# Expert stage of a decoder step: 34 passes of two 32-row half blocks, each with its own expert's weights, instead of 49 passes of one 64-row block

## The reference, cut to what matters

```python
def hier_moe(x, w_rg, b_rg, w_re, b_re, w_eg, w_eu, w_ed):   # x: 576 x 1024
    ...                                                      # group = argmax, then the best 2 of its 8 experts
    combine = jnp.sum(jax.nn.one_hot(eid, N_EXPERTS) * gate[..., None], axis=1)
    hg = jnp.einsum('nd,edf->nef', x, w_eg)                  # 32 experts, each 1024 x 256
    hu = jnp.einsum('nd,edf->nef', x, w_eu)
    hidden = jax.nn.silu(hg) * hu * combine[..., None]
    return jnp.einsum('nef,efd->nd', hidden, w_ed)           # 32 experts, each 256 x 1024
```

## Time and profile before

| | |
|---|---|
| median of 3 runs | 1352.9 us (1352.4 to 1355.35) |
| the profiled execution, its own time | 1347.98 us |
| its span, first to last instruction | 1346.0 us |
| PE busy | 1206.7 us, 90% of the span |
| mean granted TensorE clock | 0.952 |
| first transpose of the expert stage starts | 969.49 us |
| last down matmul of the stage ends | 1306.24 us |

### The profile page before, as it was taken

The page is one execution under the profiler, slowest core; times in us unless marked ns, Lnnn a source line. Parts: engine busy times, 40 slices in busy tenths (PEclk is TensorE's granted clock), DMA queues, the critical chain, the costliest instruction groups (busy, mean ns, idle before and its releaser), DMA issues.

```text
span 1346.0 us, 18797 instructions
## 1 busy us (share of the span) xinstructions
PE 1206.7 (90%) x7242; PEld 744.4 (55%) x7242; DVE 764.9 (57%) x1414; ACT 411.4 (31%) x852; POOL 570.2 (42%) x518
## 2 busy tenths in 40 slices
PE   5899999896798867788999899999998989999986
PEld 4435777685454533345666468877754545554432
DVE  1659999999888886887563134352522212221216
ACT  3630144543355465762222112231111111111110
POOL 5000096978775765757765000000233333443320
PEclk9999999998799978878999999998999999999998
DMA  9502222213565664757987320382299999999935
GB/s 329 193 28 67 63 82 76 81 52 98 148 174 167 185 191 133 252 168 250 328 266 267 133 99 32 102 323 76 84 418 413 409 395 364 366 415 416 403 113 206
DMA packets 92840, 281.46 MB, mean 209 GB/s; under 512 B 17960, under 2 KB 50552, under 8 KB 81800
## 3 DMA queue, kind: packets, MB, share of 16 engines
q1 hardware_dynamic: 54672, 165.64, 32.8%
q0 software_dynamic: 35520, 111.22, 24.7%
q10 hardware_dynamic: 2559, 3.40, 0.8%
HBM read 300.94 MB, written 23.11 MB: 241 GB/s over the span
## 4 chain that ended last, share of the span: by engine, by line
PE 49%; DVE 27%; DMA 11%; POOL 5%; issue 4%; ACT 4%; POOLq 0%; DVEq 0%; ACTq 0%; SPq 0%
PE ps L1526 9%; DVE arena L1962 6%; DVE arena L1961 5%; DVE arena L1963 5%; PE ps L1140 5%; PE ps L1550 5%; PE ps L1146 5%; POOL arena L1046 5%; PE ps L1370 4%; PE ps L1362 3%; DMA arena<-in_w_dn,arena 3%; PE ps L1228 2%; DMA arena<-scr_x,arena 2%; PE ps L1180 2%; DMA arena<-in_cache_kv,arena 2%
## 5 line engine op out<-in xcount | busy, mean ns | idle before, releaser
L1046 POOL DMA_INDIRECT arena<-in_cache_kv,arena x256 | 264.8, 1034 | 127.0 <-issue 73.7
L1140 PE MATMUL ps<-arena 128*128 128x288 f32 (+2 forms) x1120 | 294.8, 424 | 1.1 <-ACT arena L1694 1.1
L1140 PEld LDWEIGHTS ps<-arena 128*128 128x128 f32 (+1 forms) x1120 | 209.1, 189 | 84.4 <-issue 29.2
L1526 PE MATMUL ps<-arena 128*64 128x256 f32 x1568 | 189.7, 384 | 5.2 <-DMA arena<-in_w_gu 2.6
L1526 PEld LDWEIGHTS ps<-arena 128*64 128x64 f32 x1568 | 109.1, 138 | 83.8 <-issue 28.1
L1096 POOL DMA_INDIRECT scr_ypair<-arena x49 | 50.5, 1030 | 186.8 <-ACT arena L1896 168.1
L1089 POOL DMA_INDIRECT arena<-scr_x,arena x49 | 50.0, 1020 | 173.6 <-DVE arena L2343 159.0
L1617 ACT ACTIVATE arena<-ps 128x256 f32<-128x256 f32 (+5 forms) x138 | 57.9, 429 | 205.3 <-PE ps L1362 63.6
L1025 POOL TENSOR_TENSOR arena<-arena 128x816 f32<-128x816 f32 x58 | 103.0, 1775 | 17.5 <-ACT arena L1635 10.7
L1146 PE MATMUL ps<-arena 128*128 128x256 f32 (+4 forms) x544 | 107.0, 360 | 0.9 <-ACT arena L1839 0.6
L1550 PE MATMUL ps<-arena 128*64 128x512 f32 x392 | 98.9, 627 | 9.7 <-DMA arena<-in_w_dn,arena 9.7
(11 more groups left out here) (350 smaller groups left out, 1701.5 us busy)
## 6 DMA issues: line engine op xcount, KB each, us to landing
arena<-in_w_gu SPq DMA_DIRECT2D x32, 2048.0 KB, 12.5
arena<-in_w_dn SPq DMA_DIRECT2D x32, 1024.0 KB, 14.9
arena<-in_w_in SPq DMA_DIRECT2D x20, 1024.0 KB, 5.6
arena<-scr_q SPq DMA_DIRECT2D x32, 256.0 KB, 5.1
arena<-in_cache_kv,arena POOLq DMA_INDIRECT x256, 4.0
arena<-in_w_o SPq DMA_DIRECT2D x4, 1024.0 KB, 5.2
arena<-in_w_pg SPq DMA_DIRECT2D x4, 1024.0 KB, 9.2
arena<-scr_ypair SPq DMA_DIRECT2D x4, 1024.0 KB, 8.0
```

What stands on the lines that cost most here:

```text
L1046: pl.indirect_dma_start(unit_rows[:, 2 * j + t, half * H * HD:(half + 1) * H * HD], None, I["cache_kv"].rearrange("n (h d) -> (n h) d", h= ...
L1140: mm = nc.tensor.matmul(out, w[:, k], hT[:, k, a:b], start=(k == 0), stop=(k == KC - 1))
L1526: mm = nc.tensor.matmul(PS[2 + p % 2][64 * half:64 * half + 64, 0:2 * P], xT[:, p % 3, j, 64 * h:64 * h + 64], w[:, k, half, :], start=(k ...
```

## The change

The block shrinks from 64 to 32 rows, and one pass handles two blocks, each with its own weights. A block is now called a visit: 68 visits, two in each of 34 passes. There are six weight buffers of one whole expert each, and visit q always uses buffer q % 6, so pass p uses the pair (2p, 2p + 1) % 6. The blocks that are in use, sorted by expert, are numbered first, and each buffer gets a contiguous run of that numbering (`visit_blocks`): buffer 0 blocks 0 to 11, buffer 1 blocks 12 to 23, and so on. A visit whose expert is that of the visit before in the same buffer loads nothing. With these inputs 55 blocks are in use and 13 are empty.

Expert 0 is fetched early by SP into buffer 0 (one plain DMA instead of six). All other weights come by indirect DMAs of POOL, a whole expert each. Of the 68 such DMAs 32 move data, with these inputs. The number that move data in passes 0 to 33 is 1, 2, 1, 0, 2, 1, 0, 1, 1, 1, 1, 1, 1, 1, 1, 0, 0, 1, 1, 2, 1, 1, 2, 1, 0, 2, 1, 0, 1, 0, 2, 2, 0, 0. In passes 7, 9, 10, 12, 13 and 21 the one load is of the pair's second visit. (The list counts the experts that change within a buffer's run, from the rows above.)

```diff
-BLK = 64
-NOVER = (2 * N - NE) // (BLK + 1)
-NBLK = NE + NOVER
-XR = 6
+BLK = 32
+NSLOT = 6
+NBLK = -(-(2 * N + NE * (BLK - 1)) // BLK // 2)
+NVISIT = 2 * NBLK
+XR = 5
+XEARLY = 3
...
+def visit_blocks():
+
+    lengths = [len(range(j, NVISIT, NSLOT)) for j in range(NSLOT)]
+    return [sum(lengths[:q % NSLOT]) + q // NSLOT for q in range(NVISIT)]
...
                     sp.wait_ge(full, after("woS", 1))
-                    for e in range(3):
-                        load_expert(e)
-                    sp.dma_start(lng1, I["ln2_g"].rearrange("(a d) -> a d", a=1).to_broadcast([P, D])).then_inc(ln2_in, 16)
-                    sp.dma_start(lnb1, I["ln2_b"].rearrange("(a d) -> a d", a=1).to_broadcast([P, D])).then_inc(ln2_in, 16)
+                    sp.dma_start(eset[0], I["w_ex"][0:P, :]).then_inc(first_in, 16)
...
-            for e in range(3, NE):
-                sp.wait_ge(y_full, POS[("base", e - 3)] + 1)
-                load_expert(e)
...
+            def load_expert(q):
+                if q >= NSLOT:
+                    pl.wait_ge(y_full, (q - NSLOT) // 2 + 1)
+                elif q == 0:
+                    pl.wait_ge(first_in, 16)
+                pl.indirect_dma_start(eset[q % NSLOT], None, I["w_ex"],
+                                      bass.IndirectOffsetOnAxis(ap=widx[:, q:q + 1], axis=0),
+                                      bounds_check=NE * P - 1, oob_is_err=False).then_inc(expert_in[q % NSLOT], 16)
...
             for p in range(NBLK):
                 if p and p + XR - 1 < NBLK:
                     gather(p + XR - 1)
+                for q in range(2 * p + NSLOT, 2 * p + NSLOT + 2):
+                    if q < NVISIT:
+                        load_expert(q)
                 scatter(p)
...
             def up_half(p, part):
...
+                    for q in (2 * p, 2 * p + 1):
+                        pe.wait_ge(expert_in[q % NSLOT], 16 * (q // NSLOT + 1))
+                w = [up_weights(eset[q % NSLOT]) for q in (2 * p, 2 * p + 1)]
                 for k in range(4 * part, 4 * part + 4):
                     h, j = divmod(k, 4)
                     for half in range(2):
-                        mm = nc.tensor.matmul(PS[2 + p % 2][64 * half:64 * half + 64, 0:2 * P],
-                                              xT[:, p % 3, j, 64 * h:64 * h + 64], w[:, k, half, :],
-                                              start=(k == 0), stop=(k == KC - 1))
+                        for sub in range(2):
+                            r = 64 * half + BLK * sub
+                            mm = nc.tensor.matmul(PS[2 + p % 2][r:r + BLK, 0:2 * P],
+                                                  xT[:, p % 3, j, 64 * h + BLK * sub:64 * h + BLK * sub + BLK], w[sub][:, k, half, :],
+                                                  start=(k == 0), stop=(k == KC - 1))
```

More of the change, by code:

```diff
@@ L59 @@
 KXP = 8
-BLK = 64
-NOVER = (2 * N - NE) // (BLK + 1)
-NBLK = NE + NOVER
-XR = 6
-YR = 4
-EARLY = (NOVER + 1) // 2
-OVERS = [k // 2 if k % 2 == 0 else EARLY + k // 2 for k in range(NOVER)]
-def block_order():
-    order, e, o = [], 0, 0
-    while e < NE or o < NOVER:
-        for _ in range(2 if e < NE - 2 else 1):
-            if e < NE:
-                order.append(("base", e))
-                e += 1
-        if o < NOVER:
-            order.append(("over", OVERS[o]))
-            o += 1
-    return order
-BLOCKS = block_order()
-POS = {b: p for p, b in enumerate(BLOCKS)}
-def block_id(p):
-    kind, n = BLOCKS[p]
-    return n if kind == "base" else NE + n
+BLK = 32
[4 more added lines that the diff above has]
+XEARLY = 3
+YR = 4
+def visit_blocks():
+    lengths = [len(range(j, NVISIT, NSLOT)) for j in range(NSLOT)]
+    return [sum(lengths[:q % NSLOT]) + q // NSLOT for q in range(NVISIT)]
+VISITS = visit_blocks()
+assert sorted(VISITS) == list(range(NVISIT)) and NVISIT * BLK >= 2 * N + NE * (BLK - 1)
 def constants():
@@ L1242, in slot_lists @@
                 pe.wait_ge(pairs_ready, 1)
-                for half in range(2):
-                    for n in range(2 * NT):
-                        rows = TILES[n % NT][1]
-                        mm = nc.tensor.matmul(PS[4][64 * half:64 * half + 64, 0:NBLK], in_place[0:rows, n, :], in_block[0:rows, n, :],
-                                              start=(n == 0), stop=(n == 2 * NT - 1))
+                for n in range(2 * NT):
+                    rows = TILES[n % NT][1]
+                    for strip in range(4):
+                        mm = nc.tensor.matmul(PS[4][BLK * strip:BLK * strip + BLK, 0:NBLK], in_place[0:rows, n, :],
+                                              in_block[0:rows, n, strip % 2::2], start=(n == 0), stop=(n == 2 * NT - 1))
                 mm.then_inc(plist_full, 1)
@@ L2314, in blocks_and_slots @@
-                V.tensor_scalar(widx, again[:, 0:2], float(P), C["part"], ALU.mult, ALU.add).then_inc(table_ready, 1)
+                nb, incl, base, whole = [blocks[:, i, :] for i in range(4)]
+                whole = whole.bitcast(I32)
+                step(V.tensor_scalar(whole, cnt, float(BLK - 1), None, ALU.add))
+                step(V.tensor_scalar(whole, whole, 5, None, ALU.logical_shift_right))
+                step(V.tensor_copy(nb, whole))
+                step(V.tensor_tensor_scan(incl, C["ones"][:, 0:NE], nb, 0.0, ALU.mult, ALU.add))
@@ new lines, in blocks_and_slots @@
+                V.memset(turns[:, 0:1], 0.0)
+                V.memset(turns[:, 1:NSLOT], -1.0)
+                V.tensor_tensor(base, incl, nb, ALU.subtract)
+                step(V.tensor_tensor(cmp_, C["visit"].unsqueeze(2).to_broadcast([P, NVISIT, NE]),
+                                     incl.unsqueeze(1).to_broadcast([P, NVISIT, NE]), ALU.is_ge))
+                now, last = turns[:, NSLOT:], turns[:, 0:NVISIT]
+                step(V.tensor_reduce(now, cmp_, AX.X, ALU.add))
+                step(V.tensor_tensor(again, now, last, ALU.is_equal))
@@ L2315, in blocks_and_slots @@
+                step(V.scalar_tensor_tensor(again, again, float(NE), now, ALU.mult, ALU.add))
+                V.tensor_scalar(widx, again, float(P), C["part"], ALU.mult, ALU.add).then_inc(table_ready, 1)
                 rk = ranks[:, 0:NT * NE].rearrange("p (t e) -> p t e", t=NT)
-                step(V.tensor_scalar(over, rk, float(BLK), None, ALU.is_ge))
-                V.tensor_tensor(rk, rk, C["baseslot"].unsqueeze(1).to_broadcast([P, NT, NE]), ALU.add)
-                step(V.tensor_tensor(over, over, base.unsqueeze(1).to_broadcast([P, NT, NE]), ALU.mult))
@@ L2319, in blocks_and_slots @@
-                step(V.tensor_tensor(rk, rk, over, ALU.add))
+                step(V.scalar_tensor_tensor(rk, base.unsqueeze(1).to_broadcast([P, NT, NE]), float(BLK), rk, ALU.mult, ALU.add))
                 for j in range(2):
```

199 lines of the change are left out of this document (75 added, 124 removed).

## The result

The changed kernel took 1380.4 us (median of 4 runs, 1379.1 to 1383.9) against 1352.7 for the kernel before beside it, a ratio of 1.0206 with an interval of 1.0181 to 1.0230. The direction and the range of the prediction held; the size was more than twice what was forecast.

A forecast was written before the change was run, and what follows sets the result against it. The prediction took PE to bound the kernel before (310 us of passes), the DMAs close behind (304). It added 18.4 us in the stage, took off 7.2 ahead of it: 1352.9 + 11.2 = 1364 us, range 1346 to 1382.

The forecast's parts named there:

- The sign: Whole kernel: the change makes it slower, chance 0.70.
- the pass: PE in the stage: a pass in four strips stays at 6.32 us, bounds 6.3 and 6.7.
- the number of long waits: PE in the stage: about 14 waits of the first up matmul for weights, four near 12 us.
- the half clock behind each wait: PE's matmuls behind each wait for loads: they run at 1.2 GHz, a granted clock of 0.50.
- a lone load lands 11.1 us after the release: Weight loads in the stage: 3.5 us fixed plus 7.6 for bytes, so PE waits 4.8 us behind one pass of 6.3.
- The term of the waits: PE's waits for weight loads in the stage, summed pass by pass: 107.3 us.
- both should go: 7.2 us gained: Ahead of the stage: the 4.4 us wait for w_pp and 2.8 us of slow matmul records behind it vanish.
- 14 x 2.2 for the clock: PE behind the stage's 14 long waits: slow clock costs 2.2 us each, 30.8 us in all.
- Rival 4: Stage: the clock costs less, 0.9 us for each wait, stage 343.6 us, 1352.5 in all, no change; chance 0.12.
- 2 (loads land sooner): Weight loads in the stage: fixed part of 2.2 us, stage 334 us, 1343 in all, faster; chance 0.12.
- 3 (bytes): Stage: the lead doesn't matter and bytes bound it, 269 us, 1278 in all, faster; chance 0.06.
- 5 (slower in four strips): PE in the stage: a pass takes 7.7 us, stage some 373 to 378, 1382 to 1387 in all; chance 0.12.

The follow-up runs named there:

- d1: Changed kernel with two short GpSimd writes between the release of a pair's buffers and the issue of its loads; ratio 1.029 to the kernel before.
- v3: Changed kernel with fourteen waits filled by matmuls whose results nobody reads; ratio 1.022 to the kernel before, stage 361.4 us.
- v2: Changed kernel with each load in halves, each half with its own release, third visit's load behind the last of w_pp; 1292.4 us, ratio 0.958 to the kernel before.
- e1: Changed kernel with weights loaded for the first six visits alone, where the kernel before takes 1482.1 us; ratio 0.951 to it.
- r1: Changed kernel, unchanged, where the kernel before takes 1473.4 us; ratio 1.026 to it.
- v1: Changed kernel with weights loaded for the first six visits alone, where the kernel before takes 1352.4 us; ratio 0.919 to it.

## Why the prediction was half right

**Right.** The sign; the pass (6.29 us forecast as 6.32, 216.6 for all, against 217.0); the number of long waits (14 of 5 us or more, four of them 12.6 to 13.8); a lone load's landing; the busy time of PE (245, "some 250"), the DMA share (0.71, "near 0.75") and the half clock behind each wait. The 28.5 us by which the matmuls are slower answer to the 30.8 of the sum.

**The step that failed first, "a lone load lands 11.1 us after the release".** The term of the waits was mis-sized: 120.7 us instead of 107.3. The fixed part came from a row that counts from the issue, and I set it against a lead that counts from the release. Between the two, POOL's wait takes 1.0 us. The landing itself was right: the eight lone loads of the long waits landed 10.4 to 12.0 us after their issue, 11.0 on the mean. By groups: the four double waits 52.2 for 49.6, passes 22 and 31 15.9 for 14.6, the four where the load is the pair's second 26.9 for 24.4, passes 11, 17 and 28 16.7 for 14.4, pass 1 5.2 for 4.3, and five short ones, 3.7 in all, for nothing. By d1's 10 us of stage for each microsecond, the missing 1.0 us is worth some 10 of the 13.4, an estimate. The other 3 or so no run takes by themselves.

**The second, "both should go: 7.2 us gained".** I removed a queue from in front of one `w_pp` load and didn't ask what now stands in front of the last one. The three expert loads leave at 945.39 to 948.03, before it, and it landed 10.5 us after its issue. The wait moved, 4.78 us and 2.3 of slow records. Ahead of the stage the change gained 67.7 - 65.5 = 2.1 us, and that came from the slot lists, for which I had taken no change. So 5.1 of the forecast's gain wasn't there.

**The sum.** + 30.4 in the stage and - 2.1 ahead of it are + 28.3, where the forecast was + 18.4 - 7.2. The 17.1 between are 13.4 of waits less 1.4 (clock and passes together), and 5.1 ahead of the stage.

**Right in the sum, open as a cause.** "14 x 2.2 for the clock" came out as slow matmuls. What they cost the stage is another number: v3 took away 18.4 us of slow matmuls, and the stage got 6.2 shorter, or up to 15.0 if the fillers hadn't outlasted their waits. Rival 4 said that passes which wait anyway hide some slow matmuls. In passes 6 to 12 they do. Its forecast of no change in time didn't come.

**The other rivals.** 2 (loads land sooner): 10.4 to 12.0 from issue, no. 3 (bytes): not for this kernel, at a share of 0.71, yet it is near the bound in v2, beside GpSimd's pace. 5 (slower in four strips): no in the 1350 groups, and yes, in part, in the 1475 groups, by e1, and by r1, where the hidden transposes of passes 13, 14 and 15 lie 7.5 and 7.6 us apart (6.3 in the changed kernel's first profile).

The Trainium skill's page "DMA: Bandwidth & Descriptors" (Anatomy of one DMA) gives about 2.0 us plus bytes at 436 GB/s. An estimate by that is 9.2 us for such a load. The trace disagrees: 10.4 to 12.0 from issue to landing, 11.0 on the mean.

## What to carry to other kernels

When buffers rotate, count the lead from the release (the last reader's end) to the first use, and the load from that same moment: release to issue, issue to landing. The first of these is short, but it is paid at every wait (1.0 us here, some 10 in the stage). If the lead is shorter than the load, no count of bytes saves the change; give each part of a buffer its own release and its own wait. Here the stage became 82 us shorter by that, with the same loads and buffers, until the next limits (the bytes, and the engine that issues) stood in its place. When a load is taken from in front of another, look at what stands before the next one in the queue. And when you add a delay or a filler to measure a term, read from the trace what it really added: here a delay of 1.5 us added 0.75, and fillers outlasted their waits by 8.8 us.

## What the runs showed of the hardware

- The kernel before takes 1350 to 1353 us in some groups and 1473 to 1482 in others, but its stage is not longer in these (329.6 against 336.8 us). Passes of matmuls in four narrow strips are: without loads 7.7 us there and 6.3 in the 1350 groups (e1, v1). What feeds PE more slowly there I did not find out.
- From the next up half's start behind the last reader to the issue of the indirect DMA it is 1.02 us, but a write on GpSimd began 0.28 us behind it (1133.72 - 1133.44, d1).
- Six indirect DMAs issued without a pause took 7.9 us (v2), 1.3 us each, whether they moved data or not.
- Eighty matmul records of 34 columns with 32-column weights took 1.26 us, 16 ns each; forty of 49 columns with 64-column weights took 3.37, 84 ns each.
- Up records of 256 columns in four strips ran at 1.91 us for 32, 60 ns each, with two experts' weights (the 1350 groups). 64 weight loads of 32 columns in a row made it no slower there.
